# Experts of a two-block network: GpSimd instead of VectorE makes the low part of one weight load in six

## The reference, cut to what matters

```python
aff = jax.nn.softmax((h @ router_w).astype(jnp.float32), axis=-1)
vals, idx = lax.top_k(jnp.swapaxes(aff, 1, 2), cap)
xs = jax.vmap(lambda hb, ib: hb[ib])(h, idx)
hid = jax.nn.silu(jnp.einsum('becd,edf->becf', xs, w_gate)) * jnp.einsum('becd,edf->becf', xs, w_up)
out = jnp.einsum('becf,efd->becd', hid, w_down) * vals[..., None].astype(h.dtype)
return jax.vmap(lambda ob, ib: jnp.zeros((t, d), h.dtype).at[ib.reshape(-1)].add(ob.reshape(-1, d)))(out, idx)
```

## Time and profile before

| what | value |
|---|---|
| median of 3 runs | 2927.64 us (2926.36 to 2928.28) |
| the profiled execution's own time | 2919.65 us |
| its span | 2917.9 us |
| TensorE busy (matmuls) | 2316.5 us, 79% of the span |
| VectorE busy | 1713.5 us, 59% |
| ScalarE busy | 1202.0 us, 41% |
| GpSimd busy | 645.7 us, 22% |
| mean granted TensorE clock | 0.918 of full speed |

### The profile page before, as it was taken

The page is one execution under the profiler, slowest core; times in us unless marked ns, Lnnn a source line. Parts: engine busy times, 40 slices in busy tenths (PEclk is TensorE's granted clock), DMA queues, the critical chain, the costliest instruction groups (busy, mean ns, idle before and its releaser), DMA issues. The chain is left out here.

```text
span 2917.9 us, 64212 instructions
## 1 busy us (share of the span) xinstructions
PE 2316.5 (79%) x28060; PEld 1934.9 (66%) x28060; DVE 1713.5 (59%) x2450; ACT 1202.0 (41%) x2160; POOL 645.7 (22%) x568
## 2 busy tenths in 40 slices
PE   5799995877777779693498899899228999777889
PEld 5677784777676766583377777777217777655767
DVE  1555656655555527526688788888446757354652
ACT  2422112444444422133377777776242223255430
POOL 0300013545454410023101111011233444100000
PEclk8799997999999998797699999999659999899989
DMA  5222222111111115335489999999473243100032
GB/s 193 74 64 64 71 67 64 56 55 44 55 44 55 30 59 208 133 127 212 149 312 347 344 333 340 349 346 338 129 270 110 83 149 101 35 1 1 1 123 108
DMA packets 150467, 411.81 MB, mean 141 GB/s; under 512 B 10518, under 2 KB 39340, under 8 KB 150188
## 3 DMA queue, kind: packets, MB, share of 16 engines
q1 hardware_dynamic: 134700, 355.26, 34.7%
q0 software_dynamic: 10880, 39.85, 5.1%
q10 hardware_dynamic: 4608, 12.58, 1.1%
HBM read 349.95 MB, written 52.43 MB: 138 GB/s over the span
## 5 line engine op out<-in xcount | busy, mean ns | idle before, releaser
L1621 DVE TENSOR_TENSOR exp_w_lo<-exp_w,exp_w_hi 128x4096 fp32r<-128x4096 f32 x93 | 410.2, 4422 | 121.8 <-ACT exp_w_hi L1578 121.6
L1578 ACT ACTIVATE exp_w_hi<-exp_w 128x1024 fp32r<-128x1024 f32 x384 | 373.7, 1047 | 178.6 <-DMA exp_w<-in_exp_w_down_dram 95.8
L1947 PE MATMUL bank<-w_hi,h_lo 128*128 128x512 f32 (+1 forms) x448 | 175.4, 392 | 35.6 <-DMA h_lo<-h_tiles 26.7
L1916 POOL TENSOR_TENSOR w_lo<-heads_a,w_hi 128x512 fp32r<-128x512 f32 (+1 forms) x104 | 138.3, 1355 | 185.6 <-ACT w_hi L1962 185.6
L1544 PE MATMUL bank<-exp_w_hi,xsT_lo 128*128 128x512 f32 x512 | 162.0, 398 | 11.8 <-DVE exp_w_lo L1621 6.5
L1947 PE MATMUL bank<-w_lo,h_hi 128*128 128x512 f32 (+1 forms) x448 | 171.2, 382 | 0.0
L1947 PE MATMUL bank<-w_hi,h_hi 128*128 128x512 f32 (+1 forms) x448 | 170.8, 381 | 0.0
L1544 PE MATMUL bank<-exp_w_lo,xsT_hi 128*128 128x512 f32 x512 | 158.9, 392 | 0.0
L1544 PE MATMUL bank<-exp_w_hi,xsT_hi 128*128 128x512 f32 x512 | 158.3, 390 | 0.0
L793 DVE TENSOR_TENSOR w<-bank,const 128x256 f32<-128x256 f32 x200 | 75.4, 418 | 128.4 <-PE bank L902 127.9
L1512 POOL DMA_INDIRECT moe_rows<-exp_out,idxT x16 | 25.2, 1578 | 564.6 <-DVE exp_out L1672 564.6
(11 more groups left out here) (354 smaller groups left out, 6198.3 us busy)
## 6 DMA issues: line engine op xcount, KB each, us to landing
exp_w<-in_exp_w_gate_dram SPq DMA_DIRECT2D x32, 2048.0 KB, 8.6
exp_w<-in_exp_w_up_dram SPq DMA_DIRECT2D x32, 2048.0 KB, 27.6
exp_w<-in_exp_w_down_dram SPq DMA_DIRECT2D x32, 2048.0 KB, 13.4
heads_a<-in_w_in_dram SPq DMA_DIRECT2D x96, 256.0 KB, 2.7
chunk<-rkv_scratch SPq DMA_DIRECT2D x40, 512.0 KB, 4.4
ada_w_second<-in_ada_w_dram SPq DMA_DIRECT2D x8, 2048.0 KB
w_in_ring<-in_w_in_dram SPq DMA_DIRECT2D x26, 512.0 KB, 3.9
ada_w_first<-in_ada_w_dram SPq DMA_DIRECT2D x4, 2048.0 KB, 11.1
```

Source lines behind the costliest of these rows:

```text
L1578: last = act.activation(wh[:, n % RH, k, :], w[:, n % RING, k, :], ACT.Copy)
L1621: dve.tensor_tensor(wl[:, n % RH, :, :], w[:, n % RING, :, :], wh[:, n % RH, :, :], ALU.subtract).then_inc(lo_ok, 1)
L1916: pool.tensor_tensor(wl[:, q % SR, 0:width(q)], w[:, q % WR, 0:width(q)], wh[:, q % SR, 0:width(q)], ALU.subtract).then_inc(w_lo, 1)
L1947: mm = pe.matmul(g.ps[m % 4][:, 0:cols], lhs[:, t % HT, k, :], rhs[:, q % SR, 0:cols], start=(k == 0 and p == 0), stop=(k == KT - 1 and p ...
```

## The change

GpSimd now also walks over n from 1 to 96. It makes the low part of every load n >= 3 with n % 6 == 4, which is the first half of the gate matrix of experts 1 to 15 and the first half of the last down matrix: 16 loads. It waits for what VectorE's `split` waits for, and for `lo_ok` to show that all earlier low parts are made. VectorE leaves these 16 out, and ahead of each of its own low parts from load 3 on it waits for the earlier ones too. The gather of expert e+2 now comes when the up matrix of expert e is through, behind GpSimd's low part, and the scatter of expert e when its down matrix is through.

```diff
+        def on_pool(n):
+            return n >= RH and n % 6 == 4
+
...
-            for e in range(NE):
-                if e + 2 < NE:
+            for n in range(1, len(loads) + 1):
+                kind, e = tasks.get(n, ("", 0))
+                if n + 2 < len(loads) and on_pool(n + 2):
+                    pool.wait_ge(hi_ok, n + 3)
+                    pool.wait_ge(lo_ok, n + 2)
+                    pool.wait_ge(w_read, n + 3 - RH)
+                    pool.tensor_tensor(wl[:, (n + 2) % RH, :, :], w[:, (n + 2) % RING, :, :], wh[:, (n + 2) % RH, :, :],
+                                       ALU.subtract).then_inc(lo_ok, 1)
+                if kind == "up" and e + 2 < NE:
                     gather(e + 2)
-                pool.wait_ge(o_ok, e + 1)
-                if e >= 1:
-                    pool.wait_ge(added, 16 * e)
-                pool.indirect_dma_start(g.moe, bass.IndirectOffsetOnAxis(ap=g.idxT[:, e:e + 1], axis=0), o[:, e % 2, :], None,
-                                        compute_op=ALU.add).then_inc(added, 16)
+                if kind == "down":
+                    pool.wait_ge(o_ok, e + 1)
+                    if e >= 1:
+                        pool.wait_ge(added, 16 * e)
+                    pool.indirect_dma_start(g.moe, bass.IndirectOffsetOnAxis(ap=g.idxT[:, e:e + 1], axis=0), o[:, e % 2, :], None,
+                                            compute_op=ALU.add).then_inc(added, 16)
...
                 if n >= RH:
                     dve.wait_ge(w_read, n - RH + 1)
+                    dve.wait_ge(lo_ok, n)
...
-                if n + 2 < len(loads):
+                if n + 2 < len(loads) and not on_pool(n + 2):
                     split(n + 2)
```

## The result

The changed kernel takes 2986.7 us (median of 4, 2984.43 to 2988.80), the kernel before 2927.0: ratio 1.0207, 95% interval 1.0190 to 1.0225. It is 2% slower, some 60 us; the forecast was 2997, in a range of 2970 to 3023.

What follows compares the result with a forecast made beforehand. It took a closed loop through the first gate load's low part to bound the kernel: 15 links of 4.43 us plus a last 3.05 gave +69.5, 2997 us against a median of 2927.64, range 2970 to 3023.

Steps and rivals of the forecast that it cites:

- The link: First gate load's low part, which frees the buffer for load 43: 8.85 us on GpSimd against VectorE's 4.42, loop 4.43 longer.
- the 15 links of 4.43: Loads 4, 10, ..., 88 in the experts: each lengthens the loop by 4.43 us, 66.5 us together.
- part is won back: Rival, chance 0.14: gathers move their rows in the transfers' gap before load 43's data, 2.0 us each; +42, 2969 us.
- The closed loop: Expert 7's turn: seven steps from load 39's high part to load 45's sum to the whole period, 40.61 us, without slack.
- The upper bound: GpSimd's low part slowed 1.21 times by VectorE working beside it on SBUF: 10.7 us, in all +100.
- that rival: GpSimd slower in the turns than in its three earlier low parts, chance 0.12: 1.9 us more, 16 times; +100, 3027 us.
- The three rows: GpSimd's three low parts at the stage's start, 8829 to 8858 ns, taken while VectorE was busy with its top-k.
- The last turn: Load 94: GpSimd would end at 2048.93, so VectorE starts load 95's low part 3.05 us late; adds 3.05 us.

Runs made afterwards that it cites:

- the up load: The changed kernel with GpSimd making the low parts of n % 6 == 1 (second half of each up matrix) instead: 2954.64 us, ratio 1.0119 against the kernel before.

## Why the prediction was right

**The link** held. GpSimd's low part was forecast at 8.85 us and took 8.92; it is the issue of load 43 that it delays, and the share of 0.00 from 1720 to 1724 is where the forecast put it. A link as long without GpSimd gives the same loss (2994.66), the wait without it none (2924.35).

**The size** was 10 us too high: +69.5 against +59.7 by the medians. Part of that is the scatter of the times: measured again, the same change cost 67.9. That the two profiled executions differ by 69.1, nearly the forecast, is luck, since 4.4 of it lie ahead of the change. What the trace shows of the sum is 65.5 in place of 69.5. The term that was off is the 15 links of 4.43: over 12 turns each lost 3.99 although the link grew by 4.50, 5.3 us less than forecast, and what lies ahead of them and behind them took 1.3 more. The 0.5 us a turn lie in the transfers behind the late issue (means of 12 turns): load 43 is ready 9.45 us after its issue where it was 8.20, load 44 8.44 after load 43 where it was 10.03, and load 45 0.2 sooner after that. This is what the rival "part is won back" would give, at a quarter of its size, if the gather's rows move beside load 43 and no longer beside load 44; that they do is inferred from these times. 4.45 a turn were lost where the gathers were untouched.

**The closed loop** was half right. Lengthening it cost nearly in full, shortening it by 3.87 us gave 0.2, less than a measurement can tell from nothing. One turn that adds up to its period shows a chain that binds, not that it is the only one. And 40.61 was a long turn: the mean was 39.81.

**VectorE** stood still as forecast, 10.0 us each time (140.2 / 14; "some 9" was said, though the rows behind it, 0.91 + 8.85, give 9.8). But the reason given, the wait on `lo_ok`, isn't needed: without it VectorE is held all the same (9.12 us). The upper bound had the wrong engine slowed: against a low part that GpSimd has begun, it is VectorE that waits, and GpSimd stays at 8.9. The +30 us of that rival could not have come this way. The three rows by which the forecast ruled it out could not tell: beside them VectorE ran its top-k, whose operations read 16x1024 elements of one tensor, and no subtraction of two tensors. In the earlier trace rows, among short operations of VectorE, it is GpSimd that takes longer. The gathers held by a low part of VectorE and the low parts of VectorE held by GpSimd fit together with it: the engine that comes second pays.

**TensorE** was off in both waits: 5.66 ahead of the gate product where 3.5 was forecast, and 1.24 ahead of the next down product where 4.27 - 1.6 = 2.7 were to be left. The pause ahead of a down product has moved ahead of the gate product, and the lower clock behind it as well: with 0.97 us of pause ahead of its down product in place of 4.27, TensorE ran that product at its full clock and was done with it earlier, so it waited longer for GpSimd. It cost nothing here, since ScalarE's next high parts, of loads 43 to 45, each waited for a transfer and not for TensorE. The same reading, that a pause of TensorE covers what comes late before it, was a part of what failed in my expectation for the up load (34 us where none were expected); the other part is the late gate load shown there.

**The last turn and the windows**: from the last gate load's low part to the last scatter it took 72.1 us (2065.76 to 2137.88), 8.2 more than before, against 4.43 + 3.05 forecast; the DMA share was forecast at 0.86 and is 0.85.

## What to carry to other kernels

Before an operation is moved to a slower engine, find out what waits for that one instance: relief of a busy engine is worth nothing where that engine must wait for the result, and the same operation on the second half of an up matrix cost half as much. Subtractions of two SBUF operands on GpSimd and VectorE did not run side by side here, so a share given to GpSimd is time taken from VectorE at twice the price. Where transfers stand at 95% with gaps behind late issues, try smaller buffers and a deeper look-ahead; that was worth more here than any order of the work.

## What was not expected of the hardware

A VectorE subtraction with both inputs in SBUF makes no progress while GpSimd is inside one of its own: 9.12 us for 4.42 of work begun 4.12 us into GpSimd's 8.95, and 6.22 for 1.22. A gather on GpSimd is held in the same way by a low part that VectorE has begun: 4.21 or 4.99 us in place of 0.99, ending 0.81 to 0.86 us after VectorE's subtraction each time. And the same bytes in loads of 1 MB instead of 2 MB, with more of them under way, moved at 386 instead of 343 GB/s, with TensorE at its full clock in that window.
